# Who writes the diagonals of the combining matmuls: ScalarE in place of VectorE

## The chip, the cores and the metric

One core of one Trainium2 chip runs one program. The time is the device time of that core in microseconds (us), median of three runs. The engines are TensorE (PE in the profile, its weight loads PEld), VectorE (DVE), ScalarE (ACT), GpSimd (POOL) and SyncE (SP). SyncE and GpSimd issue the DMAs here.

## The reference

A decoder layer over 1024 tokens plus 16 meta tokens, D = 1024, all float32: a mixer (differential attention and a gated convolution), a residual, and then a feed-forward part with product keys, a residual and a last RMSNorm. The change lies in the feed-forward part. For each token it picks, in each of 8 heads, 16 experts of 16,384, and combines them:

```python
gate = softmax(c_top)                                   # 16 scores per token and head
act  = gelu(einsum('thkd,td->thk', u_tab[e], xt))       # one dot product per expert
w    = gate * act
y    = einsum('thk,thkd->td', w, v_tab[e])              # the sum over experts
```

## The kernel before, in words

The program has two phases. `mixer_phase` computes the mixer and ends at about 550 us of the span. `expert_phase` (from L877) does the rest, and is the one that the change touches.

**Work of the expert phase.** Tokens come in NT = 8 tiles of 128 (one token per partition). A tile has PH = 8 heads, so there are NSTEPS = 64 steps m (tile t = m // 8, head h = m % 8), and each step has TOPK = 16 experts k. One expert of one step, for all 128 tokens, is a row g = 16 m + k; there are 1024. The tables of `u` and `v` lie side by side in DRAM, so that one gathered line of 2048 floats (8 KB) holds both halves for one token, and a row g is 1 MB.

**What each engine does for a row.**
- POOL (L992): an indirect DMA gathers row g into `ring[:, g % 8]` once `combine(g - 8)` has released the slot (`b_free`). For k = 0 it also waits for the step's indices (`b_route`).
- DVE `dot(g)` (L1229): multiplies the u half with the tokens and sums into `dots[:, k]`.
- ACT (L1083): `gelu[:, k]` from `dots[:, k]`.
- DVE `diagonal(g)` (L1239): `diag[:, g % 4, :] = pairs * gelu[:, k] * gate[:, k]`. `pairs` is two 64x64 identities, one below the other, so `diag` is a pair of 64x64 diagonal matrices. It waits for the gelu, for k = 0 for the step's gates, and for `combine(g - 4)`, which frees one of the DIAGS = 4 buffers.
- PE `combine(g)` (L1345): multiplies the diagonals with the v half and adds into `acc` in PSUM; the profile shows 8 matmuls of 64x512 per row.

**Order of the work.** It is written out by hand, per engine, in program order. DVE's loop over m and k runs `dot(g)`, then a piece of the routing of a later step (`route`, top-16 searches and index arithmetic, one piece per k), at some k a piece of a norm, and last `diagonal(g - LAG)` with LAG = 2:

```python
dot(g)
if k <= 8 and m + 1 < NSTEPS:
    route(m + 1, 6 + k)
...
if g >= LAG:
    diagonal(g - LAG)
```

ACT's loop runs the gelu of row g, and behind it at certain k: `gate_exp(m + 1)` at k = 4 (L1057, an Exp; the next gelu needs its table loaded anew), copies of the next queries out of PSUM at k = 6 and 8 (L1045, L1051), at h = 4 and 5 the norm of the next tile, and at h = 0 of every tile but the first the square sums (k = 4, L1062) and the root (k = 8, L1068) of the tile before. PE runs `combine` of the row, and behind it at k = 0 to 2 eight matmul steps of the queries of step m + 2 (L1321), at k = 4 and 6 their transposes and key scores, and for h < 4 at k = 5 and 12 a piece of the output projection of the next tile (L1302). At each tile start `begin` puts the residual into `acc` (L1355). SP loads the next tile's mixer output and residual and stores a tile's output (L1009).

After the last row there is a tail: three diagonals, three combines, the last norm (L1062, L1361, L1133, L1068, L1137, L1142) and the store.

Of the kernel before, what the change touches and what calls it, by code (L numbers as in the profile page):

```python
# [9 lines left out]
ALU = mybir.AluOpType  # L10
ACT = mybir.ActivationFunctionType
# [3 lines left out]
P = 128  # L15
# [856 lines left out]
LAG = 2  # L872
# [4 lines left out]
def expert_phase(nc, shared, x, mix_dram, g2, wq, table, g_final, out):  # L877

    ctx = ExitStack()
    with ctx:  # L880
        def sb(name, shape, dt=F32):
            return ctx.enter_context(nc.sbuf_tensor(name, shape, dt))
# [4 lines left out]
        def sem(name):  # L887
            return ctx.enter_context(nc.semaphore(name))
# [30 lines left out]
        gate = [sb("gate_even", [P, TOPK]), sb("gate_odd", [P, TOPK])]  # L919
        dots = sb("dots", [P, TOPK])  # L920
        gelu = sb("gelu", [P, TOPK])
        diag = sb("diag", [P, DIAGS, HP])

        acc = [pb("acc_even", [P, D]), pb("acc_odd", [P, D])]
# [30 lines left out]
        b_free = sem("b_free")  # L955
        b_dot = sem("b_dot")
        b_gelu = sem("b_gelu")
        b_diag = sem("b_diag")
        b_lss = sem("b_lss")
        b_lsum = sem("b_lsum")  # L960
# [66 lines left out]
        def _(act):  # L1027
            def square(p):
                act.wait_ge(b_hsum, p + 1)
                if p >= 2:  # L1030
                    act.wait_ge(b_out, 64 * (p - 1))
                act.activation(xn[p % 2][:], h_next[:], ACT.Square, accum_out=nrm[:, 0:1]).then_inc(b_pss, 1)
# [33 lines left out]
            def last_root(t):  # L1066
                act.wait_ge(b_lvar, t + 1)
                act.activation(fin[:, 0, :], fin[:, 1, :], ACT.Sqrt).then_inc(b_lstd, 1)  # L1068

            square(0)  # L1070
            root(0)
            transposed(0, 0)
# [6 lines left out]
            for m in range(NSTEPS):  # L1079
                t, h = divmod(m, PH)  # L1080
                for k in range(TOPK):
                    act.wait_ge(b_dot, TOPK * m + k + 1)
                    act.activation(gelu[:, k:k + 1], dots[:, k:k + 1], ACT.Gelu).then_inc(b_gelu, 1)  # L1083
                    if k == 4 and m + 1 < NSTEPS:
                        gate_exp(m + 1)
                    if k == 6 and m + 2 < NSTEPS:
                        queries(m + 2)
                    if k == 8 and m + 2 < NSTEPS:
                        queries_t(m + 2)
                    if t + 1 < NT and h == 4 and k == 2:  # L1090
                        square(t + 1)
                    if t + 1 < NT and h == 4 and k == 6:
                        root(t + 1)
                    if t + 1 < NT and h == 5 and k in (9, 12):
                        transposed(t + 1, (k - 9) // 3)
                    if t >= 1 and h == 0 and k == 4:
                        last_square(t - 1)
                    if t >= 1 and h == 0 and k == 8:
                        last_root(t - 1)
            last_square(NT - 1)  # L1100
            last_root(NT - 1)

        @block.vector
        def _(dve):
# [124 lines left out]
                dve.tensor_tensor_reduce(ring[:, g % RING, 0:D], ring[:, g % RING, 0:D], xn[(m // PH) % 2][:], 1.0, 0.0,  # L1229
                                         ALU.mult, ALU.add, dots[:, k:k + 1]).then_inc(b_dot, 1)  # L1230

            def diagonal(g):
                m, k = divmod(g, TOPK)
                dve.wait_ge(b_gelu, g + 1)
                if k == 0:
                    dve.wait_ge(b_gate, m + 1)
                if g >= DIAGS:
                    dve.wait_ge(b_free, g - DIAGS + 1)
                dve.tensor_scalar(diag[:, g % DIAGS, :], pairs[:, 0, :], gelu[:, k:k + 1], gate[m % 2][:, k:k + 1], ALU.mult,  # L1239
                                  ALU.mult).then_inc(b_diag, 1)  # L1240

            residual(0, 0)
            residual(0, 1)
            variance(0)
# [9 lines left out]
            for m in range(NSTEPS):  # L1254
                t, h = divmod(m, PH)
                for k in range(TOPK):
                    g = TOPK * m + k
# [3 lines that stand above are left out]
                    if k == 8 and m + 1 < NSTEPS:  # L1261
                        gate_sum(m + 1)
                    if k == 9 and m + 1 < NSTEPS:
                        route(m + 1, 15)
                        gates(m + 1)
                    if k >= 10 and m + 2 < NSTEPS:
                        route(m + 2, k - 10)
                    if t + 1 < NT and h == 4:
                        if k < 2:
                            residual(t + 1, k)  # L1270
                        elif k == 5:
                            variance(t + 1)
                        elif k == 9:
                            factor(t + 1)
                        elif k == 10:
                            normalise(t + 1)
                    if t >= 1 and h == 0:
                        if k == 7:
                            last_variance(t - 1)
                        elif k == 11:  # L1280
                            last_factor(t - 1)
                        elif k == 12:
                            last_scale(t - 1)
                    if g >= LAG:
                        diagonal(g - LAG)
            for g in range(NSTEPS * TOPK - LAG, NSTEPS * TOPK):
                diagonal(g)
            last_variance(NT - 1)
            last_factor(NT - 1)
            last_scale(NT - 1)  # L1290
# [162 lines left out]
```

## Time and profile before

| | us |
|---|---|
| median of 3 runs (lowest, highest) | 3183.6 (3182.36, 3184.69) |
| the profiled execution, its time | 3180.26 |
| its span, first to last instruction | 3178.5 |
| TensorE's mean granted clock over the span | 0.833 of full |
| bytes moved by DMA | 1121.58 MB, 1073.81 MB of them on the indirect DMAs' queue |

The page of the profile gives each engine's busy time, the span in 40 slices, the chain of work that ended last, and groups of instructions by line with their mean duration. The trace gives single instructions in order of time, and the busy share of the DMA engines in any window. A share of DMA of about 1.0 says that all 16 DMA engines had packets under way throughout.

### The profile page before, as it was taken

The numbers are of one execution on the slowest core, as the hardware profiler recorded it, in microseconds if no ns is written. First come the engines' busy times: TensorE is split into PE (matmuls) and PEld (weight loads), VectorE is DVE, ScalarE is ACT, GpSimd is POOL, SyncE is SP. The second block draws the span as 40 slices with busy tenths as digits, with TensorE's granted clock in tenths as the row PEclk, the third lists the DMA queues.
The fourth block names the chain that finished last, engine by engine and source line by source line (L and its number), as shares of the span: only waits on it lengthen the run. The fifth ranks groups of instructions, "written<-read, shape, count | busy, mean of one in ns | idle before, by whom it ended". The sixth has DMA issues, their size and how long they took to land.

```text
span 3178.5 us, 35285 instructions
## 1 busy us (share of the span) xinstructions
PE 2407.4 (76%) x11880; PEld 872.3 (27%) x11880; DVE 2295.8 (72%) x5927; ACT 710.0 (22%) x1963; POOL 1147.7 (36%) x1073
## 2 busy tenths in 40 slices
PE   8998977677777777777777777767777787767776
PEld 4655554221222222222222222222222222212111
DVE  1566673677777777777777777777777777777775
ACT  3143444112121212121212121212121111211111
POOL 1000000344434444444443344444444444444443
PEclk9999987888888888887888878787897788887776
DMA  3300001999999999999999999999999999999998
GB/s 109 119 27 27 20 7 34 397 426 426 426 413 416 426 424 409 419 425 420 419 418 426 422 416 412 422 425 424 417 420 422 421 415 420 420 425 417 422 422 337
DMA packets 184956, 1121.58 MB, mean 353 GB/s; under 512 B 19520, under 2 KB 45248, under 8 KB 53584
## 3 DMA queue, kind: packets, MB, share of 16 engines
q0 software_dynamic: 147456, 1073.81, 80.9%
q1 hardware_dynamic: 37328, 45.63, 4.2%
q8 instruction: 90, 1.47, 0.2%
q14 instruction: 82, 0.67, 0.1%
HBM read 1110.97 MB, written 8.39 MB: 352 GB/s over the span
## 4 chain that ended last, share of the span: by engine, by line
DMA 49%; PE 19%; issue 7%; DVE 5%; POOL 2%; ACT 0%; DVEq 0%; SPq 0%; POOLq 0%; ACTq 0%
DMA ring<-table,e_even 25%; DMA ring<-table,e_odd 24%; PE acc_even L1345 6%; PE acc_odd L1345 6%; PE qq_ps L1321 4%; PE proj L1302 3%; POOL ring L992 2%; DVE diag L1239 1%; DVE dots L1229 0%; DVE cand_t L1189 0%; DVE ring L1229 0%; DVE hot L1208 0%; DVE hot L1202 0%; DVE top_i L1172 0%; DVE top_i L1162 0%
## 5 line engine op out<-in xcount | busy, mean ns | idle before, releaser
L1345 PE MATMUL acc_odd<-ring,diag 64*64 64x512 f32 x4096 | 712.9, 778 | 342.5 <-DVE diag L1239 334.9
L1345 PE MATMUL acc_even<-ring,diag 64*64 64x512 f32 x4096 | 690.7, 755 | 341.4 <-DVE diag L1239 334.1
L1229 DVE CUSTOM_DVE_ANT_0 ring<-ring,xn_odd 128x1024 f32<-128x1024 f32 x512 | 627.5, 1226 | 305.2 <-DMA ring<-table,e_odd 155.1
L992 POOL DMA_INDIRECT ring<-table,e_even x512 | 557.1, 1088 | 774.7 <-PE acc_even L1345 363.3
L1229 DVE CUSTOM_DVE_ANT_0 ring<-ring,xn_even 128x1024 f32<-128x1024 f32 x512 | 627.5, 1226 | 285.1 <-DMA ring<-table,e_odd 147.5
L992 POOL DMA_INDIRECT ring<-table,e_odd x512 | 558.0, 1090 | 711.5 <-PE acc_even L1345 346.4
L1083 ACT ACTIVATE gelu<-dots 128x1 f32<-128x1 f32 x1024 | 207.6, 203 | 2081.8 <-DVE dots L1229 2066.0
L1345 PEld LDWEIGHTS acc_odd<-ring,diag 64*64 64x64 f32 x4096 | 126.0, 156 | 795.2 <-DVE diag L1239 740.6
L1345 PEld LDWEIGHTS acc_even<-ring,diag 64*64 64x64 f32 x4096 | 123.3, 153 | 766.4 <-DVE diag L1239 711.3
L1321 PE MATMUL qq_ps<-wq_rest,xnT_cur 128*128 128x256 f32 x896 | 266.1, 435 | 6.5 <-DMA wq_rest<-wq 6.5
L1321 PEld LDWEIGHTS qq_ps<-wq_rest,xnT_cur 128*128 128x128 f32 x896 | 175.7, 212 | 192.3 <-issue 164.6
L1239 DVE TENSOR_SCALAR diag<-pairs,gelu,gate_even 128x64 f32<-128x64 f32 x512 | 168.8, 330 | 0.0
L1239 DVE TENSOR_SCALAR diag<-pairs,gelu,gate_odd 128x64 f32<-128x64 f32 x512 | 167.9, 328 | 0.0
L558 DVE SCALAR_TENSOR_TENSOR y<-u_pad,cpar,y 128x1024 f32<-128x1024 f32 x120 | 158.7, 1323 | 6.8 <-DVE y L558 0.9
L733 PE MATMUL proj<-xnT,w_slot 128*128 128x352 f32 x512 | 158.1, 464 | 1.4 <-DVE yc L594 1.4
L1302 PE MATMUL proj<-w_out_s,mix_t 128*128 128x512 f32 x224 | 147.6, 794 | 0.0
L733 PEld LDWEIGHTS proj<-xnT,w_slot 128*128 128x128 f32 x512 | 97.2, 192 | 55.0 <-issue 5.1
L1083 ACT ACT_TABLE_LOAD x78 | 100.1, 1283 | 1.4
L619 DVE CUSTOM_DVE_ANT_0 z<-bankA,bias 128x264 f32<-128x264 f32 (+8 forms) x112 | 52.8, 506 | 62.2 <-PE bankA L744 61.8
L1229 DVE DVE_READ_ACCUMULATOR2_ANT dots<- 128x1 f32 x1024 | 84.4, 82 | 0.0
L1302 PEld LDWEIGHTS proj<-w_out_s,mix_t 128*128 128x128 f32 x224 | 51.4, 255 | 114.5 <-issue 114.5
L1057 ACT ACT_TABLE_LOAD x64 | 82.1, 1283 | 1.4
(190 smaller groups left out, 1936.0 us busy)
## 6 DMA issues: line engine op xcount, KB each, us to landing
w_slot<-w_in SPq DMA_DIRECT2D x16, 512.0 KB, 4.0
ring<-table,e_even POOLq DMA_INDIRECT x512
ring<-table,e_odd POOLq DMA_INDIRECT x512
wq_rest<-wq SPq DMA_DIRECT2D x1, 7168.0 KB, 21.9
w_out_s<-x SPq DMA_DIRECT2D x8, 512.0 KB, 4.0
w_out_s<-w_out SPq DMA_DIRECT2D x1, 4096.0 KB, 12.9
h_next<-x SPq DMA_DIRECT2D x8, 512.0 KB, 13.8
mix_t<-mix_dram SPq DMA_DIRECT2D x7, 512.0 KB
```

The source lines that it names most:

```text
L558: dve.scalar_tensor_tensor(out=y[:], in0=u_pad[:, META + k:META + k + SEQ], scalar=cp[:, k:k + 1], in1=y[:], op0=ALU.mult, op1=ALU.add).th ...
L619: dve.tensor_tensor_reduce(z[:, i % 2, c, lo:hi], banks[3 + c][:, 0:hi - lo], bias[:, off + lo:off + hi], 1.0, NEG, ALU.add, ALU.max, zmax ...
L733: ins = pe.matmul(banks[n][:, 0:w], w_slot[:, slot, k, :], xnT[:, k, lo:lo + w], start=(k == 0), stop=(k == KC - 1))
L992: pool.indirect_dma_start(out=ring[:, g % RING, :], out_offset=None, in_=table[:, :], in_offset=bass.IndirectOffsetOnAxis(ap=e_row[m % 2][ ...
L1057: act.activation(g_exp[:], c_top[:], ACT.Exp, bias=neg_top[:], accum_out=g_sum[:, 0:1]).then_inc(b_gexp, 1)
L1083: act.activation(gelu[:, k:k + 1], dots[:, k:k + 1], ACT.Gelu).then_inc(b_gelu, 1)
L1229: dve.tensor_tensor_reduce(ring[:, g % RING, 0:D], ring[:, g % RING, 0:D], xn[(m // PH) % 2][:], 1.0, 0.0, ALU.mult, ALU.add, dots[:, k:k ...
L1239: dve.tensor_scalar(diag[:, g % DIAGS, :], pairs[:, 0, :], gelu[:, k:k + 1], gate[m % 2][:, k:k + 1], ALU.mult, ALU.mult).then_inc(b_diag, 1)
L1302: ins = pe.matmul(proj[b][:], mix_t[:, k, :], w_out_s[:, k, HALF[b]], start=(k == 0), stop=(k == KC - 1))
L1321: ins = pe.matmul(q_ps, xnT[:, k, :], w, start=(k == 0), stop=(k == KC - 1))
L1345: ins = pe.matmul(acc[t % 2][ROWS[j], HALF[i]], diag[ROWS[i], g % DIAGS, :], ring[ROWS[i], g % RING, D + j * 512:D + (j + 1) * 512], start ...
```

## The change

VectorE's `diagonal` is taken out. ScalarE gets two functions instead. `row_weight(g)` writes `weight[:, k] = gelu[:, k] * gate[:, k]` (a Copy with a per-partition scale, one element per partition). `diagonal(g)` writes `diag[:, g % 4, :] = pairs * weight[:, k]` (a Copy with a per-partition scale, 64 elements). In ScalarE's loop they stand directly behind the gelu of row g: first `row_weight(g - 1)`, then `diagonal(g - 2)`, then what stood behind the gelu before. The waits for the gates and for the free `diag` buffer move to ScalarE with them. PE still waits for `b_diag`.

```diff
@@ expert_phase, ScalarE
+            def row_weight(g):
+                m, k = divmod(g, TOPK)
+                act.wait_ge(b_gelu, g + 1)
+                if k == 0:
+                    act.wait_ge(b_gate, m + 1)
+                act.activation(weight[:, k:k + 1], gelu[:, k:k + 1], ACT.Copy, scale=gate[m % 2][:, k:k + 1]
+                               ).then_inc(b_weight, 1)
+
+            def diagonal(g):
+                act.wait_ge(b_weight, g + 1)
+                if g >= DIAGS:
+                    act.wait_ge(b_free, g - DIAGS + 1)
+                act.activation(diag[:, g % DIAGS, :], pairs[:, 0, :], ACT.Copy, scale=weight[:, g % TOPK:g % TOPK + 1]
+                               ).then_inc(b_diag, 1)
+
+            act.wait_ge(b_const, 6)
...
                     act.activation(gelu[:, k:k + 1], dots[:, k:k + 1], ACT.Gelu).then_inc(b_gelu, 1)
+                    if TOPK * m + k >= 1:
+                        row_weight(TOPK * m + k - 1)
+                    if TOPK * m + k >= LAG:
+                        diagonal(TOPK * m + k - LAG)
                     if k == 4 and m + 1 < NSTEPS:
                         gate_exp(m + 1)
...
+            row_weight(NSTEPS * TOPK - 1)
+            for g in range(NSTEPS * TOPK - LAG, NSTEPS * TOPK):
+                diagonal(g)
             last_square(NT - 1)
@@ expert_phase, VectorE
-            def diagonal(g):
-                m, k = divmod(g, TOPK)
-                dve.wait_ge(b_gelu, g + 1)
-                if k == 0:
-                    dve.wait_ge(b_gate, m + 1)
-                if g >= DIAGS:
-                    dve.wait_ge(b_free, g - DIAGS + 1)
-                dve.tensor_scalar(diag[:, g % DIAGS, :], pairs[:, 0, :], gelu[:, k:k + 1], gate[m % 2][:, k:k + 1], ALU.mult,
-                                  ALU.mult).then_inc(b_diag, 1)
...
-                    if g >= LAG:
-                        diagonal(g - LAG)
-            for g in range(NSTEPS * TOPK - LAG, NSTEPS * TOPK):
-                diagonal(g)
```

## Rows read from the trace of the kernel before

**Rows 1.** The page: busy time by engine, and DMA in 40 slices.
```profile
PE 2407.4 (76%) x11880; PEld 872.3 (27%) x11880; DVE 2295.8 (72%) x5927; ACT 710.0 (22%) x1963; POOL 1147.7 (36%) x1073
...
DMA  3300001999999999999999999999999999999998
GB/s 109 119 27 27 20 7 34 397 426 426 426 413 416 426 424 409 419 425 420 419 418 426 422 416 412 422 425 424 417 420 422 421 415 420 420 425 417 422 422 337
```
**Rows 2.** The page: the chain that ended last, by line.
```profile
DMA ring<-table,e_even 25%; DMA ring<-table,e_odd 24%; PE acc_even L1345 6%; PE acc_odd L1345 6%; PE qq_ps L1321 4%; PE proj L1302 3%; POOL ring L992 2%; DVE diag L1239 1%; DVE dots L1229 0%; DVE cand_t L1189 0%; DVE ring L1229 0%; DVE hot L1208 0%; DVE hot L1202 0%; DVE top_i L1172 0%; DVE top_i L1162 0%
```
**Rows 3.** Chain in time, 2900 to 3178 us (start, us): its longest and shortest DMA.
```profile
2983.28 12.50 DMA ring<-table,e_odd
...
3065.51 9.49 DMA ring<-table,e_odd
```
**Rows 4.** Windows: length, busy by engine, then PEclk, DMA share, GB/s.
```profile
600.00:640.00 40.00, 29.91 (x168) 9.18 (x166) 31.83 (x83) 6.75 (x22) 17.10 (x18) 0.91 1.01 426
...
1936.00:1937.00 1.00, 1.00 (x8) 0.52 (x10) 0.59 (x3) 0.22 (x1) 0.70 (x2) 1.00 0.59 180
1937.00:1938.00 1.00, 1.00 (x12) 0.31 (x8) 1.00 (x3) 0.22 (x2) 0.48 (x1) 1.00 0.89 197
```
**Rows 5.** The page: groups by line (busy, mean ns, idle before and its releaser).
```profile
L1229 DVE CUSTOM_DVE_ANT_0 ring<-ring,xn_odd 128x1024 f32<-128x1024 f32 x512 | 627.5, 1226 | 305.2 <-DMA ring<-table,e_odd 155.1
L992 POOL DMA_INDIRECT ring<-table,e_even x512 | 557.1, 1088 | 774.7 <-PE acc_even L1345 363.3
...
L1083 ACT ACTIVATE gelu<-dots 128x1 f32<-128x1 f32 x1024 | 207.6, 203 | 2081.8 <-DVE dots L1229 2066.0
...
L1239 DVE TENSOR_SCALAR diag<-pairs,gelu,gate_even 128x64 f32<-128x64 f32 x512 | 168.8, 330 | 0.0
L1239 DVE TENSOR_SCALAR diag<-pairs,gelu,gate_odd 128x64 f32<-128x64 f32 x512 | 167.9, 328 | 0.0
```
**Rows 6.** Groups by line of ACT: two that take a per-partition column as operand.
```profile
L431 ACT ACTIVATE o_all<-bankA,zinv 128x128 f32<-128x128 f32 x32 | 11.5, 359 | 0.0
...
L1057 ACT ACTIVATE g_exp<-c_top,neg_top 128x16 f32<-128x16 f32 x62 | 19.1, 308 | 0.7
```
**Rows 7.** Timeline of one ordinary row (start, us, what).
```profile
1504.10 0.07 DVE L1229 DVE_READ_ACCUMULATOR2_ANT dots<- 128x1 f32 x1
...
1504.21 0.20 ACT L1083 ACTIVATE gelu<-dots 128x1 f32<-128x1 f32 x1 [2.30 <-DVE dots L1229]
...
1504.64 0.30 DVE L1239 TENSOR_SCALAR diag<-pairs,gelu,gate_even 128x64 f32<-128x64 f32 x1
```
**Rows 8.** Timeline of the third tile's first step, k = 4 to 6.
```profile
1240.34 1.28 ACT L1057 ACT_TABLE_LOAD   x1
...
1242.71 1.24 POOL L992 DMA_INDIRECT ring<-table,e_even  x1 [1.57 <-PE acc_even L1345]
...
1243.22 0.31 DVE L1239 TENSOR_SCALAR diag<-pairs,gelu,gate_even 128x64 f32<-128x64 f32 x1
...
1244.50 0.20 ACT L1083 ACTIVATE gelu<-dots 128x1 f32<-128x1 f32 x1
1244.97 0.94 POOL L992 DMA_INDIRECT ring<-table,e_even  x1 [1.02 <-PE acc_even L1345]
...
1246.27 0.20 ACT L1083 ACTIVATE gelu<-dots 128x1 f32<-128x1 f32 x1 [1.57 <-DVE dots L1229]
1246.38 0.37 ACT L1045 ACTIVATE q_s<-qq_ps 128x256 f32<-128x256 f32 x1
```
**Rows 9.** Timeline of POOL around the dip at 1936 us: two issues that follow each other.
```profile
1928.85 0.94 POOL L992 DMA_INDIRECT ring<-table,e_odd  x1 [2.36 <-PE acc_even L1345]
1934.96 1.28 POOL L992 DMA_INDIRECT ring<-table,e_odd  x1 [5.18 <-issue]
```
**Rows 10.** Timeline of the tail: last dot's end, last gelu, last three combines.
```profile
3166.28 0.08 DVE L1229 DVE_READ_ACCUMULATOR2_ANT dots<- 128x1 f32 x1
...
3166.40 0.20 ACT L1083 ACTIVATE gelu<-dots 128x1 f32<-128x1 f32 x1 [3.21 <-DVE dots L1229]
...
3166.65 2.81 PE L1345 MATMUL acc_odd<-ring,diag 64*64 64x512 f32 x24 [1.44 <-DVE diag L1239]
```

More of the change, by code:

```diff
@@ L921, in expert_phase @@
         gelu = sb("gelu", [P, TOPK])
+        weight = sb("weight", [P, TOPK])
         diag = sb("diag", [P, DIAGS, HP])
@@ L957, in expert_phase @@
         b_gelu = sem("b_gelu")
+        b_weight = sem("b_weight")
         b_diag = sem("b_diag")
```

## The prediction, made before the changed kernel was run

> **What bounds the kernel now.** I read first the busy times and the DMA slices of the page [rows 1]. No engine is full: PE shows 76%, VectorE 72%, ScalarE 22%. The DMA row shows 9 tenths or more in every slice from the eighth to the one before the last, at 409 to 426 GB/s. Next the chain that ended last [rows 2]: 49% of it is landing of gathered rows. Then the same chain in order of time: from a gather's issue to its landing pass 9.49 to 12.50 us [rows 3]. At 426 GB/s [rows 4] a row of 1.0486 MB takes 2.46 us, so about four rows stand in the queue. That queue is the cover of everything else: 1024 rows x 2.46 us = 2521 us, and the expert phase, from about 577 us to the tail, is little longer. Last, who waits: `dot` waits for DMA (305.2 us before 512 of them), POOL's issue waits for PE (774.7 us before 512), the gelu waits for `dot` [rows 5]. An operation in the loop can cost time only if it makes POOL issue so late that the queue runs dry. That does happen a little: around 1936 us PE had fallen behind, two issues lay 6.1 us apart instead of 2.5 [rows 9], and the DMA share fell to 0.59 and 0.89 for two microseconds [rows 4].
>
> **What the change removes.** 512 x 330 ns + 512 x 328 ns = 336.7 us of VectorE [rows 5], which goes from 2296 to about 1959 us (62%). It buys nothing directly: what ends VectorE's idle time is the landing of the row, so it only waits 0.33 us longer for the same data. VectorE also loses the wait for `b_free`, behind which its next `dot` used to stand.
>
> **What it adds.** Per row, two instructions on ScalarE. Neither form exists in the loop. For `row_weight` (one element, a column as scale) the bounds are the gelu, 203 ns with one element [rows 5], and the Exp with a column as bias, 308 ns with 16 elements [rows 6]; I take 308, because it has the column. For `diagonal` (64 elements, a column) the bounds are the same 308 and 359 ns for 128 elements with a column [rows 6]; I take 333, the middle. So 1024 x (308 + 333) ns = 656 us more, ScalarE goes from 710 to about 1366 us (43%). A row's share is 0.20 + 0.31 + 0.33 = 0.84 us of 2.46 us, so it isn't a new bound.
>
> The Trainium skill, ScalarE: Activation LUTs, section What ACT_TABLE_LOAD costs, says that a column operand adds about 93 ns to 186 ns plus 0.833 ns per element. By that estimate the two would take 280 and 332 ns, and the tail below would be +0.42 us and not +0.45.
>
> **When a diagonal is ready.** Two instructions of ScalarE may start 0.11 us apart although the first lasts 0.20 (gelu and query copy in [rows 8]), so 0.09 us of each overlaps the next. The gelu starts 0.04 us behind the end of the dot [rows 7]. From the dot's end: 0.04 + 0.11 (gelu) + 0.22 (weight) + 0.33 (diagonal) = 0.70 us. Before, it is 1504.94 - 1504.17 = 0.77 us in [rows 7], as VectorE puts a routing piece first. An ordinary row thus releases PE at the same time or slightly earlier. The software pipeline (weight one row behind, diagonal two) means that ScalarE waits for its own results nowhere but in the tail.
>
> **The late one.** Behind k = 4 stands `gate_exp`: table load 1.28, Exp 0.31, its accumulator read, and another table load before the next gelu. Before, VectorE wrote a diagonal in that hole; now the diagonal of k = 3 stands behind it. At a tile start [rows 8]: the load moves from 1240.34 by 0.46 us (weight and diagonal stand before it), so the gelu goes from 1244.50 to 1244.96, and the diagonal ends 0.11 + 0.22 + 0.33 later, at 1245.62. VectorE had it at 1243.53: 2.1 us late. In the other steps the square sums (1.26 us) are missing but the dot comes 0.7 us sooner: about 1.5 us late. It happens 63 times. POOL's issue follows: the gap between two issues becomes 1244.97 + 2.1 - 1242.71 = 4.4 us at tile starts and about 3.9 us otherwise, against the 6.1 us that emptied the queue [rows 8, 9]. What covers it is the four rows in the queue; without that cover it would be 7 x 2.1 + 56 x 1.5 = 99 us. By the next row ScalarE is level again (0.84 us of work in 2.46), and where PE is itself behind, as around 1936 us, it doesn't need the diagonal sooner. I price it at nothing.
>
> **Waits that move.** Behind the `b_free` wait on ScalarE now stand the gelus, the Exp that VectorE's gates need, and the query copies that PE waits for. It holds only if PE is four rows behind; then the same wait held VectorE. The wait for the gates is met seven rows before it comes. The new wait for the constants at the start ends before ScalarE has its first input of the phase. The DMAs of SP and POOL are the same in number and order. Each of these: nothing.
>
> **The tail.** Here nothing covers. The last dot ends at 3166.36, the gelu starts at 3166.40, the first of the last three combines at 3166.65 [rows 10]. After: 3166.40 + 0.11 + 0.22 + 0.33 = 3167.06, and 0.04 to PE: 3167.10, that is +0.45 us. (Lower bound, weight 203 and diagonal 308 ns: +0.3; upper, 308 and 359 with no overlap: +0.7.) The other two diagonals are ready by 3167.8, while PE needs the third at 3167.10 + 2 x 0.94 = 3169.0.
>
> **The sum.** 3180.26 + 0.45 = 3180.7 for an execution like the profiled one. That stands 3.3 us below the median, so for the median 3183.6 + 0.45 = 3184.0. What a measurement of this kernel can tell from no change is about 0.2%, 6.4 us: no change that can be told.
>
> **Rivals.**
> 1. *Slower: the hole behind k = 4 does empty the queue.* Place: `combine` of k = 3, 63 times. It decides if the queue's reserve at that point is under the 1.5 to 2.1 us of lateness, as where query matmuls at k = 0 to 2 have already put PE behind and the projection at k = 5 follows. Price: the dip at 1936 cost (426 - 180)/426 + (426 - 197)/426 = 1.1 us [rows 4]; a dip like it at 7 tile starts, and a fifth of it in the 56 others, is 7.7 + 12.3 = 20 us: 3204. For it: the gap grows in every step. Against it: 4.4 us is under 6.1, and 9.49 us is the shortest landing of that stretch of the chain, nearly four rows. Chance 0.14.
> 2. *Faster: POOL is freed from VectorE.* A gather's issue takes 1088 ns in the mean [rows 5] and 0.94 in many single rows [rows 8, 9]. If the longer ones collide with VectorE's diagonals, issues get 0.15 us shorter, and diagonals after long routing pieces come earlier. The slices average some 421 GB/s and reach 426 [rows 1], so over 2585 us about 30 us are lost to dips; if a third comes back, 10 us: 3174. Against it: one issue's 0.15 us is covered by the same queue. Chance 0.11. The Trainium skill, SBUF — State Buffer, section Who interferes with whom, says that a `tensor_scalar` on VectorE may take the port pair that GpSimd needs to write descriptors, while ScalarE has ports of its own; by it the gathers would be issued without such stalls.
> 3. *It isn't what it says: Copy evicts the Gelu table.* Then two loads of 1.28 us per row, 0.84 + 2.57 = 3.4 us over 2.46: +960 us, 4150. Against it: the query copy follows a gelu at 1246.38 with no load [rows 8]. Under 0.01.
>
> **How the numbers follow.** Forecast 0.75, rival 1 0.14, rival 2 0.11. Range: the run-to-run spread of before (3182.4 to 3184.7), the tail's bounds, a third of each rival's size on either side, which takes in the weak forms of both: 3179 to 3192. Faster by over 0.2% (below 3177.2) 0.11, within 0.75, slower (above 3190.0) 0.14.
>
> **What would show it.** DMA slices and share as before; VectorE near 1959 us, ScalarE near 1366 with as many table loads as before; weight near 0.30 and diagonal near 0.33 us; POOL still waiting for PE; the diagonal behind `gate_exp` 1.5 to 2.1 us later with no drop of the DMA share there; the tail's first combine 0.7 us behind the last dot's end in place of 0.3. It is wrong if the share falls below 0.95 after k = 4, or if dips that are there now vanish.

## The result: 18 us faster, by fewer stalls in the row transfers

| | before | after |
|---|---|---|
| median of 5 runs, us | 3183.54 (3182.36 to 3184.69) | 3165.56 (3164.36 to 3166.92) |
| ratio of the times, 95% interval | | 0.9945 [0.9934, 0.9957] |
| profiled execution: its time, its span | 3180.26, 3178.5 | 3165.56, 3163.8 |
| first dot to last dot, starts, in that profile | 2578.5 | 2561.7 |

The changed kernel is faster by 18 us, 0.55%. The forecast was 3184.0 with a range from 3179 to 3192, so both the value and the side were wrong. The last line of the table says where the time went: the two profiled executions are 14.7 us apart in span, and between their first and last dot they differ by 16.8 us (what comes ahead of the first dot and behind the last took 2.1 us longer after the change). The gain lies in the stretch that the forecast called covered by the DMA queue.

The page of the changed kernel, with the lines that answer to [rows 1, 2, 5] (busy time, slices, the two queues that carry instructions, the chain, the groups):

```profile
PE 2385.1 (75%) x11880; PEld 864.8 (27%) x11880; DVE 2044.3 (65%) x4903; ACT 1143.5 (36%) x4011; POOL 1125.4 (36%) x1073
...
DMA  3300001999999999999999999999999999999998
GB/s 110 120 27 27 20 7 32 389 427 426 427 424 425 424 419 420 419 427 424 425 419 426 421 426 419 421 426 425 417 425 423 426 420 421 426 425 414 426 422 335
...
q8 instruction: 90, 1.47, 0.2%
q14 instruction: 90, 0.74, 0.1%
...
DMA 51%; PE 17%; DVE 6%; ACT 4%; issue 3%; POOL 1%; SPq 0%; DVEq 0%; ACTq 0%; POOLq 0%
...
L1254 DVE CUSTOM_DVE_ANT_0 ring<-ring,xn_odd 128x1024 f32<-128x1024 f32 x512 | 627.3, 1225 | 424.2 <-DMA ring<-table,e_odd 221.5
...
L994 POOL DMA_INDIRECT ring<-table,e_even x512 | 544.8, 1064 | 777.2 <-PE acc_even L1356 377.0
...
L1101 ACT ACTIVATE gelu<-dots 128x1 f32<-128x1 f32 x1024 | 207.6, 203 | 1633.2 <-DVE dots L1254 1632.3
...
L1084 ACT ACTIVATE diag<-pairs,weight 128x64 f32<-128x64 f32 x1024 | 340.2, 332 | 0.0
...
L1077 ACT ACTIVATE weight<-gelu,gate_even 128x1 f32<-128x1 f32 x512 | 142.6, 279 | 0.1
```

And two lines of the page of before that the forecast did not use:

```profile
q8 instruction: 90, 1.47, 0.2%
q14 instruction: 82, 0.67, 0.1%
```

What to see: the structure is the same. The transfers still fill every slice, the chain is still half landing, the dots still wait for rows (424.2 us before 512 of them, where [rows 5] has 305.2). Only the slices stand a little closer to 426 GB/s: from the ninth to the 39th the lowest is 414 (before 409). It isn't that a bound was lifted; the same stream of rows is interrupted less. The lines q8 and q14 are packets of program code for the engines. They are 0.1 to 0.2% of the DMA time, and the experiments below show that those of VectorE's code are the cause.

The hole behind `gate_exp` came as forecast. ScalarE in order of time, at the place of [rows 8]:

```profile
1235.32 0.20 ACT L1101 ACTIVATE gelu<-dots 128x1 f32<-128x1 f32 x1 [1.80 <-DVE dots L1254]
...
1235.96 1.28 ACT L1059 ACT_TABLE_LOAD   x1
...
1238.82 1.28 ACT L1101 ACT_TABLE_LOAD   x1
1240.12 0.20 ACT L1101 ACTIVATE gelu<-dots 128x1 f32<-128x1 f32 x1
1240.23 0.28 ACT L1077 ACTIVATE weight<-gelu,gate_even 128x1 f32<-128x1 f32 x1
1240.41 0.33 ACT L1084 ACTIVATE diag<-pairs,weight 128x64 f32<-128x64 f32 x1
```

The diagonal starts 5.1 us behind the gelu at 1235.32. Over all heads the diagonal of this place ends 1.92 us later than the dot that was executed last before it, at most 3.01; before the change it was 0.39. So it comes 1.5 us later than it did. No slice of the DMA row answers to it: the reserve of about four rows covered it.

The tail, to be laid beside [rows 10], and the same stretch in both kernels as a window (length, busy by engine, then PEclk, DMA share, GB/s):

```profile
3149.99 0.08 DVE L1254 DVE_READ_ACCUMULATOR2_ANT dots<- 128x1 f32 x1
3150.11 0.20 ACT L1101 ACTIVATE gelu<-dots 128x1 f32<-128x1 f32 x1 [1.82 <-DVE dots L1254]
3150.22 0.28 ACT L1077 ACTIVATE weight<-gelu,gate_odd 128x1 f32<-128x1 f32 x1
3150.40 0.33 ACT L1084 ACTIVATE diag<-pairs,weight 128x64 f32<-128x64 f32 x1
...
3150.78 0.30 PEld L1356 LDWEIGHTS acc_odd<-ring,diag 64*64 64x64 f32 x8 [2.14 <-ACT diag L1084]
```
```profile
3150.50:3155.00 4.50, 3.90 (x24) 1.08 (x24) 0.00 (x0) 1.13 (x5) 0.00 (x0) 0.72 0.00 0
```

Before, the window over the last three combines reads:

```profile
3166.50:3170.00 3.50, 2.81 (x24) 0.82 (x24) 0.54 (x3) 0.58 (x2) 0.00 (x0) 1.00 0.00 0
```

The last combines start at 3150.78, 0.71 us behind the dot's end, where before it was 0.29: +0.42 us, forecast +0.45. They then take 3.90 us and not 2.81. The granted clock in these windows is 0.72 against 1.00, so partly at the lower level of 1.2 GHz; the matmuls are the same.

### The profile page after: what moved, and what is told of

Same layout as the page of the kernel before. It is cut to its first block, busy times and chain, and to the rows that moved or that the text cites. A ratio compares the mean times of both kernels' runs of the same rounds, so it can differ in the third digit from the quotient of the medians.

```text
span 3163.8 us, 36373 instructions
## 1 busy us (share of the span) xinstructions
PE 2385.1 (75%) x11880; PEld 864.8 (27%) x11880; DVE 2044.3 (65%) x4903; ACT 1143.5 (36%) x4011; POOL 1125.4 (36%) x1073
## 4 chain that ended last, share of the span: by engine, by line
DMA 51%; PE 17%; DVE 6%; ACT 4%; issue 3%; POOL 1%; SPq 0%; DVEq 0%; ACTq 0%; POOLq 0%
DMA ring<-table,e_even 25%; DMA ring<-table,e_odd 25%; PE acc_odd L1356 6%; PE acc_even L1356 6%; DVE ring L1254 5%; PE qq_ps L1332 4%; PE proj L1313 2%; ACT weight L1077 1%; ACT diag L1084 1%; POOL ring L994 1%; DMA wq_rest<-wq 1%; ACT L1059 0%; ACT gelu L1101 0%; ACT L1101 0%; ACT g_exp L1059 0%
## 5 line engine op out<-in xcount | busy, mean ns | idle before, releaser
L1254 DVE CUSTOM_DVE_ANT_0 ring<-ring,xn_odd 128x1024 f32<-128x1024 f32 x512 | 627.3, 1225 | 424.2 <-DMA ring<-table,e_odd 221.5
L994 POOL DMA_INDIRECT ring<-table,e_even x512 | 544.8, 1064 | 777.2 <-PE acc_even L1356 377.0
L994 POOL DMA_INDIRECT ring<-table,e_odd x512 | 548.0, 1070 | 718.5 <-PE acc_odd L1356 350.0
L1084 ACT ACTIVATE diag<-pairs,weight 128x64 f32<-128x64 f32 x1024 | 340.2, 332 | 0.0
L1077 ACT ACTIVATE weight<-gelu,gate_even 128x1 f32<-128x1 f32 x512 | 142.6, 279 | 0.1
L1077 ACT ACTIVATE weight<-gelu,gate_odd 128x1 f32<-128x1 f32 x512 | 142.6, 278 | 0.1
L1313 PE MATMUL proj<-w_out_s,mix_t 128*128 128x512 f32 x224 | 127.9, 699 | 0.0
## 6 DMA issues: line engine op xcount, KB each, us to landing
ring<-table,e_even POOLq DMA_INDIRECT x512, 10.9
```

The lines of the kernel that those rows point to most:

```text
L994: pool.indirect_dma_start(out=ring[:, g % RING, :], out_offset=None, in_=table[:, :], in_offset=bass.IndirectOffsetOnAxis(ap=e_row[m % 2][ ...
L1077: act.activation(weight[:, k:k + 1], gelu[:, k:k + 1], ACT.Copy, scale=gate[m % 2][:, k:k + 1]).then_inc(b_weight, 1)
L1084: act.activation(diag[:, g % DIAGS, :], pairs[:, 0, :], ACT.Copy, scale=weight[:, g % TOPK:g % TOPK + 1]).then_inc(b_diag, 1)
L1313: ins = pe.matmul(proj[b][:], mix_t[:, k, :], w_out_s[:, k, HALF[b]], start=(k == 0), stop=(k == KC - 1))
```

## The experiments

Each kernel ran in five rounds beside the kernel before on the same chip; the ratios are to the kernel before. In the diffs, minus and plus are against the kernel named. The expectations go by letters. **A**: VectorE's order was to blame; a routing or norm piece stood ahead of a diagonal, made PE and POOL late, and the queue ran dry. **B**: it is VectorE's load that slows the transfers, by ports that it and GpSimd would both need (B1, rival 2 of the forecast) or by its work in some other way (B2). Later **C**: it is the number of VectorE's instructions, whatever they do, since their code is fetched over a DMA engine that is last with each row; **T**, VectorE's time; **S**, that the diagonal must be written elsewhere.

The changed kernel a second time gives the scatter.

> The changed kernel itself once more, on the chip of the three beside it. 3165 us within 3 if the 18 us are a property of the kernel; 3172 or more would say that much of the spread between the variants is that of chips and executions.

3164.42 us (3163.34 to 3166.28), 0.9946 [0.9932, 0.9959]. The gain repeats.

**Is it the order on VectorE?** Three kernels keep the diagonal on VectorE and put it ahead of the pieces. Against before:

```diff
                     dot(g)
+                    if g >= LAG:
+                        diagonal(g - LAG)
                     if k <= 8 and m + 1 < NSTEPS:
...
-                    if g >= LAG:
-                        diagonal(g - LAG)
```

> Diagonals stay on VectorE, but each is written directly behind the dot, ahead of the routing and norm pieces. Theory A (before, the diagonals stood behind VectorE's own norm and routing pieces, and the releases of ring slots came late there; the change took them out of that queue): at least the changed kernel's gain, 3155 to 3167 us, and the dips of DMA at the tile starts go. Theory B (VectorE's diagonal writes themselves hold up GpSimd's gathers, wherever they stand): they stand here as often as before, so 3180 to 3184 us.

3179.12 us (3177.53 to 3182.57), 0.9993 [0.9984, 1.0002].

The same move, but only ahead of the norm pieces:

> Diagonals stay on VectorE, behind the routing piece as before, but ahead of the pieces of the two norms (which occur at h = 4 and at h = 0 only). In the trace of before, the dips at h = 0 lose 11.6 us and after the change 5.2 us. Theory A, with the norm pieces as its seat: 3175 to 3178 us (6 to 8 us of the 18). If the routing pieces are as much to blame, it stays above that; theory B: 3183 us.

3182.24 us (3177.08 to 3185.2), 0.9998 [0.9989, 1.0007].

The first move with `LAG = 1`, so that a row's ring slot comes free one row earlier:

> As the diagonal directly behind the dot, and of the row before (LAG = 1) in place of two before: every ring slot comes free one row (2.46 us) sooner, so about five rows stand in the queue and not four. If what the dips cost is the queue running short (both theories' common ground), nearly all 37 us of the dips of before go: 3145 to 3155 us. If the dips come from the memory side, no more than the diagonal placed first alone.

3178.87 us (3176.58 to 3182.3), 0.9991 [0.9982, 1.0]. From issue to landing a row now takes 13.6 to 13.7 us by the page, where the move alone has 11.7, so nearly one row more is in the queue, and nothing comes of it. The order on VectorE is worth 3 us at most, which can't be told from nothing here. Theory A falls as the cause of the 18 us, and with it any theory by which the queue runs dry for want of issued rows. The trace of before says the same of the dip at 1936 us: through it the rows go on landing 2.44 to 2.49 us apart, with one step of 2.63 behind it, some 0.2 us lost. What is lost is lost while rows stand in the queue.

**Is it VectorE's work?** An operation whose result nothing reads is added to the changed kernel, once a row:

```diff
+                    if g >= LAG:
+                        dve.wait_ge(b_spare, g - LAG)
+                        dve.tensor_scalar(spare[:], pairs[:, 0, :], iota_f[:, 0:1], iota_f[:, 1:2], ALU.mult,
+                                          ALU.mult).then_inc(b_spare, 1)
```

> The changed kernel, and VectorE again executes a tensor_scalar of 128x64 with two column operands behind each row, into a tile nobody reads. Theory A: nobody waits for it, 3165 us within 3. Theory B: VectorE's load and its collisions with GpSimd are back, 3180 us.

3174.21 us (3168.95 to 3178.93), 0.9974 [0.9964, 0.9984]: half of the gain is gone. So it is something about VectorE's own stream. The next three ask whether it is the ports. The unread operation on 63 elements in an uneven shape:

> As the changed kernel with the unread tensor_scalar on VectorE (3174.2 us), but of 63 elements read as 3 x 21 and written as 63, so that it can't be cut in two halves. Theory B1 (the write holds ports that GpSimd needs for its gathers): 3166 us. Theory B2 (VectorE is simply busier): 3174 us, as before.

3173.2 us (3169.93 to 3176.65), 0.9977 [0.9967, 0.9987]. Then the kernel before with its diagonal written in another form, with two tensors as input, at the old place and directly behind the dot:

```diff
-                dve.tensor_scalar(diag[:, g % DIAGS, :], pairs[:, 0, :], gelu[:, k:k + 1], gate[m % 2][:, k:k + 1], ALU.mult,
-                                  ALU.mult).then_inc(b_diag, 1)
+                dve.scalar_tensor_tensor(out=diag[:, g % DIAGS, :], in0=pairs[:, 0, :], scalar=gelu[:, k:k + 1],
+                                         in1=gate[m % 2][:, k:k + 1].to_broadcast([P, HP]), op0=ALU.mult,
+                                         op1=ALU.mult).then_inc(b_diag, 1)
```

> The kernel before, at its old place in VectorE's order, but the diagonal is a scalar_tensor_tensor whose second input is the gate column, broadcast, in place of a tensor_scalar with two columns. Theory B1: about 3174 us, half of the gain. Theory B2: 3182 us.

3181.33 us (3179.78 to 3183.86), 0.9999 [0.999, 1.0008].

> The same form, directly behind the dot. There the tensor_scalar gave 3179.1 us, and the gathers' issues took 1232 ns in the mean, as they met a dot and a diagonal in a row. Theory A plus B1 (late diagonals and the ports, 8 us each): 3165 to 3168 us. Theory A alone: 3174 us. Neither: 3179 us.

3181.48 us (3177.76 to 3186.49), 1.0 [0.9991, 1.0009]. The form of the operation changes nothing in either direction, which speaks against B1. Whether these forms really leave the ports alone is shown by no trace; what rules B1 out is that waits alone, with no operation at all, have the same cost, as the runs further down show.

**Size of the work.** The unread operation, once with one element and once with 512 (`spare[:]` from `w_out_s[:, 0, 0:512]`):

> The changed kernel with the unread VectorE operation of the two dummy runs shrunk to one element per partition: the same number of instructions, waits and semaphore increments, but 1/64 of the data. Theory C: as the first dummy, 3173 to 3175 us. Theory B2 (data read and written in SBUF): 3165 to 3167 us. Theory T (time on VectorE): the fixed part of an operation's time is most of the 128x64 operation's, so 3171 to 3174 us.

3175.13 us (3172.27 to 3179.93), 0.9977 [0.9968, 0.9986].

> The changed kernel with that unread VectorE operation grown to 512 elements per partition, 128x512 read and written, one instruction as before. Theory C: 3173 to 3175 us, as the dummy of 64 elements. Theory B2: eight times the data of the dummy that cost 9 us, well above 3190 us. Theory T: some 0.3 to 0.5 us more VectorE time per row than the small dummy; if 0.3 us of VectorE time per row is worth 9 us, 3185 to 3195 us.

3174.2 us (3171.25 to 3176.74), 0.9973 [0.9963, 0.9984]. The group of this run's page shows how big the added work is:

```profile
L1303 DVE TENSOR_SCALAR spare<-w_out_s,iota_f 128x512 f32<-128x512 f32 x1022 | 578.3, 566 | 0.0
```

VectorE stands at 2533.7 us (80%) in this run, 238 us more than in the kernel before, and the kernel is still 0.27% faster than before. 262 ns and one element cost the same 9 to 10 us as 566 ns and 512 elements. VectorE's busy time and its data count for nothing; B2 and T fall.

**Instructions that do no work at all.** Four waits on a semaphore that has long had its value, behind each dot, and the same on ScalarE behind each gelu:

```diff
                     dot(g)
+                    for _ in range(4):
+                        dve.wait_ge(b_const, 6)
```

> The changed kernel, and directly behind each of the 1024 dots VectorE executes four more waits on a semaphore that has long had its value: no arithmetic, no tile read or written, only 4096 more instructions in VectorE's stream. Theory C, that each piece of VectorE's program has to be fetched by a packet that takes its turn on one of the DMA engines that also bring the table rows, and that VectorE's packets lie on the DMA engine that is last: the dummy of one instruction with its wait added 8 packets of 8 KB and 9 us, so 32 more packets cost some 36 us, about 3200 us, a ratio of 1.011. Theory B2, that it is VectorE's work on SBUF that slows the row transfers, and not its instructions: 3165 us, ratio to the kernel before 0.9945, as the changed kernel. Theory T, that it is the time that VectorE's own stream is held up between a dot and the next: the waits hold it for perhaps 0.1 to 0.2 us a row, so between 3166 and 3175 us.

3183.17 us (3181.77 to 3185.17), 1.0002 [0.9993, 1.0011].

> The changed kernel with the same four waits behind each gelu in ScalarE's stream instead. Theory C with one DMA engine for each compute engine's program: ScalarE's packets lie on a DMA engine that runs ahead, so 3165 us (within 3 us); if all program packets lie on the slowest DMA engine, some 36 us more, as for VectorE. Theory B2: 3165 us.

3165.05 us (3162.73 to 3166.04), 0.9945 [0.9931, 0.9958].

The waits on VectorE take back the whole gain; on ScalarE they cost nothing. Both pages have the same line, 16 packets more than the changed kernel:

```profile
q14 instruction: 106, 0.87, 0.1%
```

The expectation of C, 36 us, was twice too high, as the program that is built joins the four waits into two instructions: the trace has 2048 more on VectorE, and 16 packets, not 32. Between these two kernels, run on the same chip, lie 18.1 us, 8.8 ns per instruction of VectorE.

**Can the kernel before be made faster with all its work left on VectorE?** With as many diagonal buffers as ring rows the wait for a free buffer is implied by the row's landing, and can go:

```diff
-DIAGS = 4
+DIAGS = 8
...
-                if g >= DIAGS:
-                    dve.wait_ge(b_free, g - DIAGS + 1)
```

> The kernel before with its diagonals still written by VectorE, but with eight diagonal buffers in place of four, as many as the ring has rows, so that the wait for the combining matmuls ahead of each diagonal says nothing that the landed row has not said and is left out. The same arithmetic on every engine; VectorE executes 1024 semaphore instructions fewer. Theory C (VectorE's instruction count, 9 us per 1024, whatever they do): 3174 us, ratio 0.997. Theory S, that only writing the diagonal somewhere else brings the gain: 3183 us, ratio 1.000.

3173.64 us (3170.65 to 3175.99), 0.9978 [0.9969, 0.9987]. The page has VectorE at 2297.6 us, where before had 2295.8, with the same 5927 counted instructions; it has 75 packets in place of 82:

```profile
q14 instruction: 75, 0.61, 0.0%
```

The kernel before had 3181.9 us on the same chip, so this is 8.3 us for 957 instructions, nearly half of the change's gain, for waits alone. S falls.

**Whose code counts?** Four such waits per row on TensorE and on GpSimd, in the changed kernel:

> The changed kernel with four more satisfied waits on TensorE behind each row's matmuls. If only VectorE's program lies on the last DMA engine (theory C): 3165 us. If it is any engine's program but ScalarE's: up to 18 us more.

3166.48 us (3161.04 to 3169.04), 0.9949 [0.9936, 0.9963]; here it is q8 that grows, from 90 to 98 packets of 16 KB.

> The changed kernel with four more satisfied waits on GpSimd ahead of each row's issue. Theory C: 3165 us, unless GpSimd's program comes over the same DMA engine as VectorE's: then up to 18 us more, 3183 us.

3164.03 us (3162.08 to 3165.6), 0.9947 [0.9933, 0.996]; q14 grows to 106. In both, nothing is lost that can be told.

**The times against the count.** Instructions per engine are counted from the trace's records, semaphore instructions included (the page's x leaves those out):

| kernel | VectorE instr. | others against the changed kernel | q14 packets | median, us | steps over 3.1 us |
|---|---|---|---|---|---|
| before | 7456 | ScalarE -3133 | 82 | 3183.5 | 70 |
| before, the diagonal placed otherwise or in another form (five kernels) | 7456 | ScalarE -3133 | 82, 83 | 3178.9 to 3182.2 | 65 to 71 |
| four waits on VectorE | 7459 | | 106 | 3183.2 | 65 |
| before without the free wait | 6499 | ScalarE -3133 | 75 | 3173.6 | 63 |
| changed, with the unread operation of 1, 63, 64, 512 elements | 6433 | | 98 | 3175.1, 3173.2, 3174.2, 3174.2 | 64, 62, 62, 70 |
| changed kernel, two sets of runs | 5411 | | 90 | 3165.6, 3164.4 | 49, 48 |
| changed, `LAG = 1` | 5411 | | 90 | 3164.2 | 43 |
| four waits on ScalarE | 5411 | ScalarE +2048 | 106 | 3165.1 | 55 |
| four waits on TensorE | 5411 | TensorE +2048 | 90 | 3166.5 | 47 |
| four waits on GpSimd | 5411 | GpSimd +2048 | 106 | 3164.0 | 45 |
| sum on ScalarE, `LAG` 2 and 1 (below) | 4387 | ScalarE +2048 | 98 | 3182.9, 3170.6 | 67, 73 |

The sets ran on different chips, on which the kernel before had 3181.8 to 3183.5 us. In every kernel but the last two the time follows the second column and no other: (3183.5 - 3165.6) / (7456 - 5411) = 8.8 ns per VectorE instruction; the free waits give 8.6, the unread operations of 63, 512 and 1 element 8.6, 9.0 and 9.9 against a kernel at 3164 to 3165 us on the same chip. 2048 waits bring 16 packets of 8 KB, so a packet holds 128 instructions, and a packet on VectorE costs 1.1 us. The change takes 2045 instructions from VectorE: a diagonal and a semaphore instruction per row.

**What one packet does.** The last column counts, in each profile, the steps from the start of one dot to the next that are over 3.1 us; the ordinary step is 2.44. (Not all of them are code, and a step close to 3.1 falls on either side by chance.) Such a step in the kernel before (timeline of VectorE, the dots alone; start, us):

```profile
1283.62 1.23 DVE L1229 CUSTOM_DVE_ANT_0 ring<-ring,xn_even 128x1024 f32<-128x1024 f32 x1 [0.59 <-DMA ring<-table,e_odd]
...
1286.06 1.23 DVE L1229 CUSTOM_DVE_ANT_0 ring<-ring,xn_even 128x1024 f32<-128x1024 f32 x1 [0.83 <-DMA ring<-table,e_odd]
...
1289.48 1.23 DVE L1229 CUSTOM_DVE_ANT_0 ring<-ring,xn_even 128x1024 f32<-128x1024 f32 x1 [1.36 <-DMA ring<-table,e_odd]
...
1291.92 1.23 DVE L1229 CUSTOM_DVE_ANT_0 ring<-ring,xn_even 128x1024 f32<-128x1024 f32 x1 [0.38 <-DMA ring<-table,e_odd]
```

and the DMA queues of the window 1286 to 1290 us:

```profile
DMA packets 230, 1.70 MB, mean 424 GB/s; under 512 B 23, under 2 KB 23, under 8 KB 23
...
q0 software_dynamic: 229, 1.69, 100.6%
q14 instruction: 1, 0.01, 0.5%
```

Steps of 2.44, then one of 3.42 with a packet of code in it, and 2.44 again: the dot waits for the landing, 0.98 us longer, and the time isn't made up. In that window the DMA still moved 424 GB/s. A row comes in 16 parts, and the trace has the landing of each. At an ordinary landing of the kernel before, the last part comes 1.5 us behind the last but one (median over the rows). At one such step, at 1392 us, the last part landed 3.42 us behind that of the row before, but the fifteenth 2.44 and the first 2.45. One part of the row was held up, and the other 15 were not. In this kernel 44 rows land 3.35 to 3.5 us behind the one before; of the 38 whose parts are all on record, 29 look like that. There are 45 such steps with four waits on VectorE, 40 without the free wait, 32 in the changed kernel, and 3 with four waits on ScalarE. So it is the row that lands late, and not VectorE that stands without instructions.

In this kernel such steps come about every 51 us (dots at 1289, 1342, 1392, 1441, 1496, 1546); in the one with four waits on VectorE also about every 51 to 53 us; without the free wait every 60; in the changed kernel every 75 (1299, 1374, 1447, 1522, 1599, 1673). Between first and last dot VectorE executes 6343, 5389 and 4304 instructions (before, without the free wait, changed); by their count 128 of them last 2578.5 x 128 / 6343 = 52 us, 61 and 76 us. The late steps come at the pace of VectorE's code. One of those of the changed kernel:

```profile
1518.16 1.23 DVE L1254 CUSTOM_DVE_ANT_0 ring<-ring,xn_even 128x1024 f32<-128x1024 f32 x1 [0.81 <-DMA ring<-table,e_odd]
...
1521.57 1.23 DVE L1254 CUSTOM_DVE_ANT_0 ring<-ring,xn_even 128x1024 f32<-128x1024 f32 x1 [2.02 <-DMA ring<-table,e_odd]
```

ScalarE's packets (the changed kernel has about as many of them as of VectorE's) have no such step. But with 2048 instructions more on ScalarE its own packets, every 48 us, show steps of 3.1 us, as here at 1276, and VectorE's shrink (at 1445 the step is 2.59):

```profile
1274.86 1.23 DVE L1256 CUSTOM_DVE_ANT_0 ring<-ring,xn_even 128x1024 f32<-128x1024 f32 x1 [0.87 <-DMA ring<-table,e_odd]
...
1277.99 1.23 DVE L1256 CUSTOM_DVE_ANT_0 ring<-ring,xn_even 128x1024 f32<-128x1024 f32 x1 [1.49 <-DMA ring<-table,e_odd]
```

This fits a row that is complete only when the last of its 16 parts has come, with VectorE's code on the DMA engine that is last, and ScalarE's on another that has some 18 us to spare over the whole phase (16 packets of 1.1 us) and in this run has just caught up. The landings of the parts bear it out. The distance from the last part to the last but one is 1.3 us in the median of the changed kernel and 0.7 with four waits on ScalarE. Just ahead of the step at 1278 us it was 0.24 us; at the step the last part came 3.13 us behind that of the row before, the fifteenth 2.44. So the held-up part had not been the last one; it lost about 1 us, of which 0.24 was to spare. Which DMA engine carried which packet is recorded nowhere, so that each engine's code has its own DMA engine stays an inference. Of DMA engines that are last the Trainium skill, DMA: Bandwidth & Descriptors, section Latency and other measured facts, says that two of the 16 are usually slower than the rest in traces, and ties this to transfers whose descriptors GpSimd writes, with a cause that it calls a best guess. The 1.5 us above agree that one is last by a clear distance; no run here can show which two, and if VectorE's code goes over one of them.

**A version that beats both?** The dot as a plain product on VectorE (one instruction, not two), and its sum on ScalarE, in the changed kernel:

```diff
-                dve.tensor_tensor_reduce(ring[:, g % RING, 0:D], ring[:, g % RING, 0:D], xn[(m // PH) % 2][:], 1.0, 0.0,
-                                         ALU.mult, ALU.add, dots[:, k:k + 1]).then_inc(b_dot, 1)
+                dve.tensor_tensor(ring[:, g % RING, 0:D], ring[:, g % RING, 0:D], xn[(m // PH) % 2][:], ALU.mult
+                                  ).then_inc(b_dot, 1)
...
+                    act.activation(ring[:, g % RING, 0:D], ring[:, g % RING, 0:D], ACT.Copy,
+                                   accum_out=dots[:, k:k + 1]).then_inc(b_sum, 1)
```

> The changed kernel, and ScalarE also adds up the products: VectorE's dot becomes a plain product (one instruction a row, not two, about the same 1.2 us), ScalarE sums the 1024 products into the dot (perhaps 1.0 to 1.2 us a row more, which takes it from 36% to over 70% of the span). Theory C: 1024 VectorE instructions fewer, 9 us, so 3156 us, if ScalarE's new queue costs nothing. Rival: with the sum, the table loads and the exponential ScalarE falls behind by several us once a head, the ring's rows come free later, the DMA queue runs dry, and it is slower than the changed kernel: 3170 us or more, with rows issued later behind each gate_exp.

3182.85 us (3174.27 to 3186.7), 0.9997 [0.9988, 1.0006]. VectorE executes 4387 instructions, and it is as slow as before. Its page:

```profile
L1103 ACT ACTIVATE ring<-ring 128x1024 f32<-128x1024 f32 x1024 | 1078.1, 1053 | 611.1 <-DVE ring L1259 608.5
...
ring<-table,e_even POOLq DMA_INDIRECT x512, 9.8
```

From issue to landing 9.8 us are left where the changed kernel has 10.9: the sum holds each row 1.2 us longer, and the queue is shorter by that. So here the reserve may count. One row of lag less should give it back:

> The run in which ScalarE also sums the products, with each diagonal written one row behind its dot and not two, so that a ring row comes free about one row (2.45 us) earlier. The run with two rows of lag had a median of 9.8 us from a row's issue to its landing where the changed kernel has 10.9 to 11.2, and came out at 3183 us. If that lost reserve in the DMA queue is what ate the gain: with the lag back to one the median is 12 us or more, and the 1024 VectorE instructions fewer show as 3156 us, within 4 us. If something else did (ScalarE's load, the table load and exponential once a head): 3170 us or more.

3170.6 us (3167.44 to 3172.16), 0.9962 [0.9948, 0.9975].

> The control for that run: the changed kernel, with each diagonal one row behind its dot. Its reserve in the queue is one row more than it needs, so 3165 us, ratio 0.9945, unless the reserve matters here as well: then below 3160 us.

The control: 3164.18 us (3161.96 to 3169.79), 0.9945 [0.9932, 0.9959].

With the sum and one row of lag the median from issue to landing is 11.8 us. The lag gives back 12 us and is worth nothing without the sum, so the reserve does count there. The 3156 of theory C is not reached. A part of that can be told: this kernel has ScalarE at 7416 instructions, as many as the run with four waits on ScalarE, where ScalarE's packets had become late ones at 3165 (the last part of a row is only 0.4 to 0.5 us behind the last but one in both kernels with the sum); by that, fewer instructions on VectorE can't bring it lower. What the other 5 us are was not settled. None of the kernels run is faster than the changed one by more than the scatter.

## Why the prediction was wrong

- **The step that failed** stands under what the change removes: VectorE's 336.7 us of diagonals "buys nothing directly". As busy time that was right: a run with more VectorE time than before (80%) is still 9 us faster than before. But an instruction has a second cost, its code, which holds up the landings that the forecast took as given. The price of 8.8 ns per instruction, taken from the four waits alone, makes the 2045 instructions of the change 18 us, which is the gain. That term was not in the sum; the forecast priced what leaves VectorE at nothing.
- The bound was read too coarsely. "Four rows stand in the queue" covers what happens ahead of the queue. It does not cover what stands in the queue itself, and the packets of code do. The forecast even had the place: some 30 us lost to dips in 2585 us. It took them for late issues and gave a third of them to another cause. The dip at 1936 us, its measure of what a late issue costs (1.1 us), had cost the landings only some 0.2 us: a drop of the mean DMA share is not yet time. (Its row in [rows 9] also names no wait for PE, but "issue", that is no wait that the profile shows. And the eighth slice has 397 GB/s; the 409 to 426 hold from the ninth on.)
- Rival 2 (faster, 3174, by GpSimd's freed ports) had the side, but not the mechanism. POOL's issues did get shorter, 1088 to 1064 ns, not by 0.15 us, and they still waited for PE as before (777.2 us before 512 of them, against 774.7); a diagonal or an unread operation in another form made no difference; and waits alone, which write nothing, cost as much.
- Rival 1 (the hole behind `gate_exp` empties the queue): the lateness came as worked out, 1.5 to 2.1 us forecast, 1.6 in the mean, and 1.92 - 0.39 = 1.5 measured, and cost nothing that can be seen. Right to price it at nothing.
- Rival 3 (table evicted) did not happen: 78 table loads ahead of the gelu, as before.
- ScalarE's two instructions: forecast 308 and 333 ns, measured 279 and 332; the other estimate that the forecast gives, 280 and 332 ns with +0.42 us for the tail, was the better one. The sum of the busy time was off, 1366 us forecast and 1143.5 measured: the page counts a moment in which two instructions of an engine overlap once, and the 0.09 us of overlap was used for the readiness and not for the busy time. The same on VectorE: 1959 forecast, 2044.3 measured.
- The tail: +0.45 forecast, +0.42 measured to the first combine.
- The band of 0.2% for what can be told was right: the gain of 0.55% lies outside it and repeats. With dips of some 30 us seen and not explained, 0.11 for faster was little.

## What to carry to other kernels

In this kernel, a long unrolled program that gathers from memory at full rate, the code streams too. Look at the queues marked "instruction" on the page, and at the steps between two landings. A regular extra that comes once per 128 instructions of one engine points at that engine's code. It shrinks when waits are dropped or instructions move to an engine whose code is not on the late path; that wider operations, fewer in number, would do the same follows from the count and was not tried. Dropping one redundant wait per row was worth some 8 us here, about what one added operation per row cost, whatever its size.

An experiment that adds a thing (an unread operation, a satisfied wait) to the faster kernel told the causes apart better than those that rearranged the slower one.

## What the runs showed of the hardware that was not expected

- A packet of 8 KB of VectorE's code, for which the trace's record has about 0.31 us, holds up the landing of one row by 0.98 us. Why it is three times its record was not tried.
- 2048 instructions more are 16 packets of 8 KB in q14 (VectorE, ScalarE, GpSimd) and 8 packets of 16 KB in q8 (TensorE): 64 bytes each. The Trainium skill, Vector Engine (DVE) Microarchitecture Reference, section 1.2 Instruction fetch and dispatch (NX sequencer), gives that width for VectorE's instructions; the counts agree.
- 2048 instructions more cost 18 us if they are VectorE's, and nothing that can be told (within 2 us of the changed kernel) if they are ScalarE's, GpSimd's or TensorE's.
- One late part holds up a row while the DMA goes on at 424 GB/s: neither the share nor the rate of a window shows the loss, the landings do.
- With one row more in the queue the spread between the first and the last part of a row's landing grows (3.5 us in the kernel before, 6.2 in the mean in the kernel with `LAG = 1` and the diagonal first; the last part comes 1.5 and 4.2 us behind the last but one), and the rate does not: the parts that are ahead get further ahead, and the last one comes no sooner.
